# Latent attention of a two-block network: queries and key roots issued one pair ahead, probabilities normalised before the value product

## The chip, the cores and the metric

One core of a Trainium2 chip runs the whole program. The metric is device microseconds of one execution; lower is better. TensorE (PE in the profile) multiplies and writes PSUM, VectorE (DVE) and ScalarE (ACT) read and write both memories, GpSimd (POOL) reads and writes SBUF alone, SyncE (SP) issues the weight transfers.

## What is computed

The reference chains two decoder blocks over 256 tokens of width 1024 (16 meta tokens are put ahead in the first). The first block is a state-space layer, an MLP, a latent attention layer and an MLP; the second has an mLSTM, two cross-attentions, a stick-breaking attention and two gated MLPs. The change lies in the latent attention:

```python
def mla_mixer(h, w_in, q_a_g, w_q_b, kv_a_g, w_kv_b, q_norm_g, k_norm_g, w_out):
    q_lat, kv_lat, k_pe = jnp.split(h @ w_in, [MLA_Q_RANK, MLA_Q_RANK + MLA_KV_RANK], axis=-1)
    q = (rms_norm(q_lat, q_a_g) @ w_q_b).reshape(bsz, L, MLA_HEADS, MLA_QK)
    kv = (rms_norm(kv_lat, kv_a_g) @ w_kv_b).reshape(bsz, L, MLA_HEADS, MLA_NOPE + MLA_V)
    k_nope, v = jnp.split(kv, [MLA_NOPE], axis=-1)
    k = jnp.concatenate([k_nope, jnp.broadcast_to(k_pe[:, :, None, :], ...)], axis=-1)
    q = rms_norm(q, q_norm_g)
    k = rms_norm(k, k_norm_g)
    ...
        sc = jnp.einsum('bqhd,bkhd->bhqk', q[:, s:e], k[:, :e]).astype(jnp.float32) * scale
        mask = jnp.arange(e)[None, :] <= jnp.arange(s, e)[:, None]
        p = jax.nn.softmax(jnp.where(mask, sc, -jnp.inf), axis=-1).astype(v.dtype)
        outs.append(jnp.einsum('bhqk,bkhd->bqhd', p, v[:, :e]))
    o = jnp.concatenate(outs, axis=1).reshape(bsz, L, MLA_HEADS * MLA_V)
    return o @ w_out
```

There are 16 heads with 64 + 32 query and key columns and 64 value columns, a query rank of 384 and a key-value rank of 256; 272 tokens are keys, 256 are queries.

## The kernel before

Each engine has its own program, written out by hand; engines meet only at counting semaphores, which the code names by event (`q.wait_ge(*kw[h])` waits until head h's keys are weighed). Every weight block goes the same way: SP loads it into one of four RAW buffers, ScalarE rounds it to WH, VectorE writes the rest WL = RAW - WH, and TensorE multiplies by both. `PLAN` fixes the order of the blocks for all engines: eight key blocks `wk`, two value blocks `wv`, sixteen query blocks `wqb` (one a head), eight output blocks `mlao`. ScalarE rounds three blocks ahead of its place in the plan (LEAD), VectorE two (LEAD_LO), so a late engine holds back the split of later blocks. A WH and WL buffer is free once the block four back has been used.

Keys stage (`pe_mla`, first loop over c). TensorE makes one 128x272 key block (two heads); VectorE writes both heads' 64 rows to `Kt`, multiplied by the latent root `RKV`; ScalarE squares the block, and `pe_ksum` adds the squares of a head over its rows. VectorE turns the rope part of the keys (`dve_rope_keys`) ahead of the first block, and POOL copies it to all 16 heads in one instruction (`pool_mla`). The token roots of the query latent (`dve_columns(q, "q", ...)`) follow on VectorE in the first block.

Values stage. Six groups of six matmuls of 512 columns, each taken out of PSUM by VectorE (`dve_value`).

Loop over pairs of heads, t = 0 to 10, with `pairs(t)` giving up to four pairs at once: the new pair t (queries, sums of squared queries, key roots), the pair t-1 (scores, row maxima, exponentials), the pair t-2 (probabilities transposed, value product) and t-3 (output transposed back). A key root is a selector times two rows of roots, RKH and RKL, which fills a bank with the root of a head on all partitions; VectorE then multiplies the head's keys by it (`kw`). The value product has the transposed probabilities standing and 64 value columns moving, so its result lies by tokens; VectorE divides it by the row sums (`on`) and TensorE transposes it (`pe_out_transposed`). Only after the last pair do the output blocks `mlao` begin.

## Time and profile before

| | |
|---|---|
| median of 3 runs | 1812.93 us (1812.3 to 1818.2) |
| profiled execution | 1816.08 us, of which the span in the trace is 1814.3 us |
| TensorE busy | 1728.0 us (95%) |
| VectorE, ScalarE, POOL busy | 1193.6, 934.8, 316.0 us |
| latent attention, first key block to last output block | about 534.8 to 699.8 us |

The span of the trace is divided in the page into 40 slices of some 45 us; the latent attention fills slices 12 to 16 (of 1 to 40). Busy matmul time counts overlapping matmuls and matmuls at a lowered clock alike, so the granted clock (PEclk, 1.0 is 2.4 GHz and 0.5 is 1.2 GHz) has to be read beside it.

### The profile page before, as it was taken

What the parts mean: (1) busy time and instruction counts of PE and PEld (TensorE: products, weight loads), DVE (VectorE), ACT (ScalarE), POOL (GpSimd) and SP (SyncE); (2) the same over time, 40 slices, a digit from 0 to 9 for tenths busy, and PEclk for the clock granted to TensorE, in tenths of its full rate; (3) what the DMA queues carried; (4) which work ended last, traced back from release to release, by engine and by line L of the source; (5) the groups of instructions that cost most, each with busy time, mean ns of one, the idle gap of its engine ahead of it and who ended that gap; (6) DMA issues with size and microseconds to landing.
All of it is one profiled execution on the core that took longest, in us unless ns stands there. A gap on an engine that the chain in (4) does not pass through costs nothing.

```text
span 1814.3 us, 33107 instructions
## 1 busy us (share of the span) xinstructions
PE 1728.0 (95%) x13396; PEld 1659.1 (91%) x13396; DVE 1193.6 (66%) x2054; ACT 934.8 (52%) x1640; POOL 316.0 (17%) x281
## 2 busy tenths in 40 slices
PE   6999999999988999999999999999989999989997
PEld 6999889999986989999988999999989998889997
DVE  5899987555576446555766675776666766466665
ACT  5677765544443445544655444544445654354443
POOL 0000001233420002333211100000241211010025
PEclk8999999999998779999999999999999999999998
DMA  5333334555522116555533544455553343335553
GB/s 186 120 114 105 117 103 140 163 176 173 179 79 79 44 57 189 194 187 186 164 116 117 180 146 129 140 183 187 183 169 116 113 156 117 99 123 175 188 179 109
DMA packets 76328, 257.49 MB, mean 142 GB/s; under 512 B 8464, under 2 KB 12560, under 8 KB 75920
## 3 DMA queue, kind: packets, MB, share of 16 engines
q1 hardware_dynamic: 76176, 255.37, 43.9%
q8 instruction: 107, 1.75, 0.4%
q14 instruction: 45, 0.37, 0.1%
HBM read 254.29 MB, written 1.05 MB: 141 GB/s over the span
## 4 chain that ended last, share of the span: by engine, by line
PE 78%; DVE 11%; ACT 5%; issue 4%; POOL 1%; DMA 0%; POOLq 0%; DVEq 0%; ACTq 0%; SPq 0%
PE pb L140 77%; DVE WL L159 2%; DVE TMP L171 2%; DVE SCR L171 2%; DVE SCR L159 2%; PE pb L143 1%; ACT SCR L149 1%; ACT L156 1%; POOL SCR L159 1%; ACT WH L149 1%; DVE HNL L171 1%; ACT TMP L149 1%; ACT Rbuf L149 0%; ACT SCR L150 0%; DVE MX L180 0%
## 5 line engine op out<-in xcount | busy, mean ns | idle before, releaser
L140 PE MATMUL pb<-HNH,WH 128*128 128x256 f32 (+1 forms) x2176 | 632.8, 291 | 3.6 <-DVE WL L159 3.5
L140 PE MATMUL pb<-HNH,WL 128*128 128x256 f32 (+1 forms) x2176 | 621.7, 286 | 0.0
L140 PE MATMUL pb<-HNL,WH 128*128 128x256 f32 (+1 forms) x2176 | 621.2, 285 | 0.0
L159 DVE TENSOR_TENSOR WL<-RAW,WH 128x1024 fp32r<-128x1024 f32 (+4 forms) x514 | 602.5, 1174 | 6.8 <-ACT WH L149 6.1
L149 ACT ACTIVATE WH<-RAW 128x1024 fp32r<-128x1024 f32 (+4 forms) x514 | 507.4, 989 | 170.5 <-PE pb L140 169.0
L140 PE MATMUL pb<-ASH,WH 128*128 128x256 f32 (+1 forms) x1632 | 479.0, 294 | 3.2 <-DVE ASL L171 1.8
L140 PE MATMUL pb<-ASH,WL 128*128 128x256 f32 (+1 forms) x1632 | 469.3, 288 | 0.0
L140 PE MATMUL pb<-ASL,WH 128*128 128x256 f32 (+1 forms) x1632 | 468.8, 287 | 0.0
L140 PEld LDWEIGHTS pb<-HNH,WH 128*128 128x128 f32 x2176 | 415.6, 191 | 10.4 <-issue 4.7
L140 PEld LDWEIGHTS pb<-HNH,WL 128*128 128x128 f32 x2176 | 415.6, 191 | 0.0
L140 PEld LDWEIGHTS pb<-HNL,WH 128*128 128x128 f32 x2176 | 414.2, 190 | 1.1
L140 PEld LDWEIGHTS pb<-ASH,WH 128*128 128x128 f32 x1632 | 315.7, 193 | 10.6 <-issue 5.3
L140 PEld LDWEIGHTS pb<-ASL,WH 128*128 128x128 f32 x1632 | 315.0, 193 | 1.0
L140 PEld LDWEIGHTS pb<-ASH,WL 128*128 128x128 f32 x1632 | 315.7, 193 | 0.0
L140 PE MATMUL pb<-SCR 128*64 128x128 f32 (+11 forms) x928 | 136.2, 319 | 15.5 <-DVE SCR L171 9.5
L140 PEld LDWEIGHTS pb<-SCR 128*128 128x128 f32 (+5 forms) x928 | 105.7, 173 | 36.1 <-DVE SCR L171 11.2
L159 DVE TENSOR_TENSOR ASL<-TMP,ASH 128x256 fp32r<-128x256 f32 (+1 forms) x108 | 46.4, 430 | 109.2 <-ACT ASH L149 109.2
L140 PE MATMUL pb<-SQ,cp 128*128 128x256 f32 (+2 forms) x274 | 85.6, 428 | 33.5 <-ACT SQ L149 24.0
L159 POOL TENSOR_TENSOR SCR<-SCR,TMP 128x256 f32<-128x256 f32 x48 | 59.9, 1248 | 311.7 <-DVE TMP L159 311.7
L159 POOL TENSOR_TENSOR X<-X,TMP 128x272 f32<-128x272 f32 (+1 forms) x64 | 96.4, 1507 | 87.9 <-DVE TMP L159 87.9
L159 DVE TENSOR_TENSOR TMP<-pb,Rbuf 128x256 f32<-128x256 f32 (+1 forms) x112 | 47.9, 428 | 94.8 <-PE pb L140 94.8
L149 ACT ACTIVATE ASH<-TMP 128x256 fp32r<-128x256 f32 (+1 forms) x108 | 45.5, 422 | 117.2 <-DVE TMP L159 67.6
(136 smaller groups left out, 1484.8 us busy)
## 6 DMA issues: line engine op xcount, KB each, us to landing
RAW<-in_w_gu SPq DMA_DIRECT2D x88, 512.0 KB, 4.1
RAW<-in_w_up SPq DMA_DIRECT2D x64, 512.0 KB, 3.5
RAW<-in_w_down SPq DMA_DIRECT2D x64, 512.0 KB, 3.6
RAW<-in_w_ssd SPq DMA_DIRECT2D x48, 512.0 KB, 3.5
RAW<-in_w_xkv SPq DMA_DIRECT2D x32, 512.0 KB, 3.5
RAW<-in_w_mlin SPq DMA_DIRECT2D x24, 512.0 KB, 3.5
RAW<-in_w_fd SPq DMA_DIRECT2D x32, 384.0 KB, 3.0
RAW<-in_w_sbqkv SPq DMA_DIRECT2D x24, 512.0 KB, 3.9
```

The source lines that it names most:

```text
L140: return self.eng.matmul(o, l, r, start=start, stop=stop, skip_group_check=skip) if self.eng else Nothing()
L143: return self.eng.transpose(o, i, ident) if self.eng else Nothing()
L149: return self.eng.activation(o, i, f, bias=bias, scale=scale)
L156: self.eng.preload_act_table_set(name)
L159: return self.eng.tensor_tensor(o, a, b, op) if self.eng else Nothing()
L171: return self.eng.scalar_tensor_tensor(out=o, in0=a, scalar=s, in1=b, op0=op0, op1=op1)
```

## The change

- Plan: the first two query blocks come ahead of the value blocks.
- Keys are no longer multiplied by the latent root when they leave PSUM. One head is copied by VectorE and the other by ScalarE, and the latent root is multiplied into the row of key roots instead. The rope part is multiplied by its inverse (`kpe("inverse")`, `"scaled"`), cut into four steps that stand behind the first four key blocks on VectorE, and POOL copies it in eight pieces, after a 48x272 memset of RKP.
- RKH and RKL become one 48-row tile RKP (rows 0 to 15 and 32 to 47), so a key root is one matmul.
- The loop runs over t = 0 to 7. In one turn TensorE does the scores of pair t, the two query blocks of pair t+1, the transposes of pair t-1, the value product of pair t-2, and the sums and key roots of pair t+1. The sums lie in bank 3 instead of bank 2, so the scores wait for `qss` (they have been read).
- The probabilities are divided by their sums on POOL (`nrm`), 288 and 544 columns a pair, before they are transposed.
- The value product has the values standing and the probabilities moving (256 and 128 columns), and its result lies by features: no `on`, no `pe_out_transposed`.
- PT2 is copied by VectorE instead of ScalarE; PT1 and PT2 have two buffers. The mask is added by one matmul a head instead of two. The row maxima are scaled a head at a time, and so the exponentials of one head start ahead of the other's maxima.
- The last two pairs' transposes and value products are laid between parts of the first three output blocks (`pe_chunks`).

```diff
-    p += [("wk", 0, c) for c in range(8)] + [("wv", 0, k) for k in range(2)]
-    p += [("wqb", 0, h) for h in range(16)]
+    p += [("wk", 0, c) for c in range(8)] + [("wqb", 0, h) for h in range(2)] + [("wv", 0, k) for k in range(2)]
+    p += [("wqb", 0, h) for h in range(2, 16)]
...
         def pe_ksum(q, c):
             if c == 0:
-                q.wait_ge(*rms["kv"])
+                q.wait_ge(*kpe["inverse"])
...
         def pe_scores(q, p):
+            q.wait_ge(*qd[p])
+            q.wait_ge(*qss[p])
...
         def pe_transposed(q, p):
             P = PP[:, p % 2, :]
+            q.wait_ge(*nrm[p])
...
+            q.matmul(o[:, 0:256], vmt[0:32, p, :], PT2[0:32, p % 2, 256:512], True, False, True)
+            for e in range(2):
+                vc = 128 * p + 64 * e
+                q.matmul(o[64 * e:64 * e + 64, 0:256], vtk[:, 0, vc:vc + 64], PT1[:, p % 2, 256 * e:256 * e + 256], False,
+                         False, True)
...
+            for t in range(8):
+                pe_scores(q, t)
+                if t < 7:
+                    pe_query(q, 2 * t + 2)
+                if t:
+                    pe_transposed(q, t - 1)
+                if t < 7:
+                    pe_query(q, 2 * t + 3)
+                if t:
+                    pe_transposed_rest(q, t - 1)
+                if t < 7:
+                    pe_key_root(q, 2 * t + 2)
+                if t > 1:
+                    pe_outputs(q, t - 2)
+                if t < 7:
+                    pe_query_sums(q, t + 1)
+                    pe_key_root(q, 2 * t + 3)
...
+            part(0, 0, 5)
+            pe_outputs(q, 6)
+            part(1, 0, 5)
+            part(0, 5, 6)
+            pe_transposed(q, 7)
+            pe_transposed_rest(q, 7)
+            part(1, 5, 6)
+            part(2, 0, 6)
+            pe_outputs(q, 7)
...
+            for t in range(8):
+                dve_root(q, t)
+                if t > 2:
+                    dve_out(q, t - 3)
+                if t < 7:
+                    dve_block(q, "wqb", 0, 2 * t + 2, T2)
+                else:
+                    dve_split(q, AT["mlao", 0, 0])
+                for e in range(2):
+                    dve_max(q, t, e)
+                if t < 7:
+                    dve_query(q, t + 1)
+                if t:
+                    dve_transposed(q, t - 1)
+                if t < 7:
+                    dve_weigh_key(q, 2 * t + 2)
+                    dve_block(q, "wqb", 0, 2 * t + 3, T2)
+                    dve_weigh_key(q, 2 * t + 3)
+                dve_recip(q, t)
...
         def pool_mla(q):
-            q.wait_ge(*kpe["twice"])
-            q.copy(Kt[64:128, :, :], bc(kpr[64:128, 1, :], 16)).then_inc(*kfill(0))
+            q.mset(RKP[:, :].bitcast(F32), 0.0).then_inc(*rkz(0))
+            q.wait_ge(*kpe["scaled"])
+            for p in range(8):
+                q.copy(Kt[64:128, 2 * p:2 * p + 2, :], bc(kpr[64:128, 1, :], 2)).then_inc(*kfill(p))
+            q.wait_ge(*kfill[7])
+            for p in range(8):
+                P = PP[:, p % 2, :]
+                r = MX[:, p % 2, 12:16].rearrange("p (e n) -> p n e", n=2)
+                q.wait_ge(*rsd[p])
+                for n, (c0, w) in enumerate(SEGS):
+                    d = P[:, 288 * n:288 * n + 2 * w].rearrange("p (e k) -> p e k", e=2)
+                    t = q.tt(d, d, bl(r[:, n, :], w), ALU.mult)
+                t.then_inc(*nrm(p))
```

How the rows move is shown at three places. On TensorE in the loop, from the second query block of a turn to the next scores; L143 rows are transposes, `SCR 128x256`, `64x256` and `64x128` are the value product, `cp,SQ 128x1` the sums of squared queries:

```order
+L143 MATMUL pb<-cp,SCR 128x128 x2
+L143 MATMUL pb<-cp,SCR 32x128 x2
+L140 MATMUL pb<-RKP,RSEL 128x272
+L140 MATMUL pb<-SCR 128x256
+L140 MATMUL pb<-SCR 64x256 x2
+L140 MATMUL pb<-SCR 64x128 x2
 L140 MATMUL pb<-cp,SQ 128x1 x4
-L140 MATMUL pb<-RKH,IDR 128x272
-L140 MATMUL pb<-RKL,IDR 128x272
-L140 MATMUL pb<-SCR 128x128
-L140 MATMUL pb<-SCR 128x64 x2
```

The value product stood behind the sums and a key root; now it stands ahead of the sums, and what follows the sums is one key root (the next row, RKP again) and then the next pair's scores.

On VectorE at the start of the keys stage; `SCR 64x272 <- pb` takes a head's keys out of PSUM, the rows `TMP<-SCR,cp` and `SCR<-SCR,TMP` are rope steps:

```order
+L174 COPY SCR<-pb 64x272
+L171 SCALAR_TENSOR_TENSOR TMP<-pb,Rbuf 64x272
 L165 TENSOR_SCALAR SCR<-SCR,cp 64x272
+L159 TENSOR_TENSOR WL<-RAW,WH 128x256
+L174 COPY SCR<-pb 64x272
 L159 TENSOR_TENSOR TMP<-SCR,cp 32x272
 L159 TENSOR_TENSOR SCR<-SCR,cp 32x272
+L159 TENSOR_TENSOR WL<-RAW,WH 128x256
+L174 COPY SCR<-pb 64x272
 L159 TENSOR_TENSOR SCR<-SCR,TMP 32x272
```

The rope steps stood in one piece ahead of all key blocks; now a split and a copy of a key block stand between them.

On POOL, from the last norm ahead of the layer to the first squares behind it (six of the eight pairs' rows left out):

```order
-L174 COPY SCR<-SCR 64x4352
+L186 MEMSET RKP 48x272
+L174 COPY SCR<-SCR 64x544 x8
+L159 TENSOR_TENSOR SCR<-SCR 128x288
+L159 TENSOR_TENSOR SCR<-SCR 128x544
```

One long copy became eight short ones, and POOL has two multiplications a pair that it did not have.

## Rows read from the trace of the kernel before

**Rows 1.** The page: busy time, and the clock in 40 slices.

```profile
PE 1728.0 (95%) x13396; PEld 1659.1 (91%) x13396; DVE 1193.6 (66%) x2054; ACT 934.8 (52%) x1640; POOL 316.0 (17%) x281
...
PEclk8999999999998779999999999999999999999998
```

**Rows 2.** Windows: each engine's busy time in six stretches of the layer.

```profile
core 0: us, PE busy (x) PEld busy (x) DVE busy (x) ACT busy (x) POOL busy (x), PEclk, DMA share, GB/s
534.79:559.41 24.62, 15.36 (x78) 9.24 (x76) 20.31 (x42) 8.73 (x21) 4.06 (x1) 0.79 0.29 91
559.41:569.27 9.86, 9.86 (x38) 6.38 (x37) 6.74 (x13) 1.82 (x4) 0.00 (x0) 0.83 0.15 42
569.27:579.66 10.39, 8.01 (x50) 7.35 (x49) 5.09 (x13) 3.16 (x8) 0.00 (x0) 0.84 0.24 76
579.66:659.40 79.74, 77.37 (x470) 71.28 (x469) 39.67 (x121) 37.96 (x114) 0.00 (x0) 0.80 0.17 55
659.40:673.08 13.68, 11.67 (x61) 9.98 (x61) 2.92 (x10) 4.28 (x14) 0.00 (x0) 0.75 0.00 0
673.08:699.80 26.72, 26.72 (x202) 26.57 (x201) 15.19 (x24) 13.71 (x23) 3.62 (x3) 0.89 0.47 143
```

**Rows 3.** Waits and timeline, TensorE's longest wait and the rows under it.

```profile
PE pb L140 <- DVE WL L159: 6.1, 1, 6.1
...
539.43 4.06 POOL L174 COPY SCR<-SCR 64x4352 f32<-64x4352 f32 x1 [25.47 <-DVE SCR L174]
...
539.92 3.58 DVE L171 SCALAR_TENSOR_TENSOR TMP<-TMP,SCR 128x2 f32<-128x2 f32 x1
```

**Rows 4.** Timeline: start, duration; a key block and its sum, two value matmuls.

```profile
549.89 0.63 PE L140 MATMUL pb<-SQ,cp 128*16 128x272 f32 x2
550.45 0.39 PE L140 MATMUL pb<-ASH,WH 128*128 128x272 f32 x1
...
566.01 0.40 PE L140 MATMUL pb<-WH,ASL 128*128 128x512 f32 x1
566.25 0.40 PE L140 MATMUL pb<-WL,ASH 128*128 128x512 f32 x1
```

**Rows 5.** Timeline of TensorE in the loop: starts give each part's pace.

```profile
584.70 0.39 PE L140 MATMUL pb<-ASH,WH 128*128 128x256 f32 x1
...
586.93 1.04 PE L143 MATMUL pb<-cp,SCR 128*128 128x128 f32 x8
...
625.15 1.17 PE L140 MATMUL pb<-SCR 128*128 128x128 f32 x8
...
627.35 1.00 PE L140 MATMUL pb<-cp,SQ 96*128 96x1 f32 x8
628.61 0.39 PE L140 MATMUL pb<-RKH,IDR 16*128 16x272 f32 x1 [0.26 <-DVE SCR L159]
...
628.96 2.71 PE L140 MATMUL pb<-SCR 32*128 32x128 f32 x16
631.60 0.59 PE L140 MATMUL pb<-RKH,IDR 16*128 16x272 f32 x1
...
632.34 0.58 PE L140 MATMUL pb<-ASH,WH 128*128 128x256 f32 x1
...
636.35 1.95 PE L143 MATMUL pb<-cp,SCR 128*128 128x128 f32 x10
```

**Rows 6.** Timeline: VectorE in the loop, and POOL beside VectorE elsewhere.

```profile
591.81 0.50 DVE L171 SCALAR_TENSOR_TENSOR SCR<-SCR,cp,pb 128x272 f32<-128x272 f32 x1 [0.60 <-PE pb L140]
...
626.63 0.65 DVE L180 TENSOR_REDUCE SCR<-pb 128x1 f32<-128x144 f32 x2 [1.30 <-PE pb L140]
...
868.79 0.91 POOL L159 TENSOR_TENSOR X<-X,TMP 128x256 f32<-128x256 f32 x1 [0.24 <-DVE TMP L159]
869.03 1.76 DVE L159 TENSOR_TENSOR WL<-RAW,WH 128x1024 fp32r<-128x1024 f32 x1
...
944.13 1.00 POOL L159 TENSOR_TENSOR SCR<-SCR,cp 128x384 f32<-128x384 f32 x1 [2.75 <-ACT SCR L149]
```

More of the change, by code:

```diff
@@ L323, in pe_block, with pe_chunks @@
             q.wait_ge(*lo[i])
+            pe_chunks(q, i, T, xs, 0, KC[name])
+        def pe_chunks(q, i, T, xs, k0, k1):
             o = bank_of(i)[:, 0:T]
-            kc = KC[name]
-            for k in range(kc):
+            kc = KC[PLAN[i][0]]
+            for k in range(k0, k1):
                 xh, xl, ready = xs[k]
@@ new lines, in pe_mla, with part @@
+            ox = as_chunks("o", 8, 8, T2)
+            first = []
+            for m in range(3):
+                first.append(q.block("mlao", 0, m))
+            def part(m, k0, k1):
+                if k0 == 0:
+                    pe_bank_free(q, first[m])
+                    q.wait_ge(*lo[first[m]])
+                pe_chunks(q, first[m], T2, ox, k0, k1)
+            part(0, 0, 5)
[3 more added lines that the diff above has]
+            pe_transposed(q, 7)
@@ L1339, in act_mla @@
                 q.activation(SQ[:, c % 3, 0:T1], b, ACT.Square).then_inc(*eva(i))
+            for e in range(2):
+                act_block(q, "wqb", 0, e, T2)
             act_block(q, "wv", 0, 0, 512)
@@ new lines, in dve_transposed, with dve_recip @@
+        def dve_transposed(q, p):
+            q.wait_ge(*tp2[p])
+            if p > 1:
+                q.wait_ge(*pv[p - 2])
+            q.copy(PT2[:, p % 2, 0:256], banks[6][:, 0:256])
+            q.copy(PT2[0:32, p % 2, 256:512], banks[6][0:32, 256:512]).then_inc(*pt2(p))
+        def dve_recip(q, p):
+            M = MX[:, p % 2, :]
+            q.wait_ge(*ex[2 * p + 1])
+            if p > 1:
+                q.wait_ge(*nrm[p - 2])
+            q.recip(M[:, 12:16], M[:, 8:12]).then_inc(*rsd(p))
@@ L1447, in dve_mla @@
                     dve_columns(q, "kv", 2, 3)
-            dve_rope_keys(q)
+            kv16 = row(RKV, T1)[0:16, :]
             for c in range(8):
                 i, b = dve_block(q, "wk", 0, c, T1)
-                if c == 0:
+                q.wait_ge(*use[i])
+                q.copy(Kt[0:64, 2 * c, :], b[0:64, :]).then_inc(*evd(i))
+                dve_rope_keys(q, c)
+                if c == 5:
                     dve_columns(q, "q", 0, 2)
```

404 lines of the change are left out of this document (195 added, 209 removed), and 2 rows, old and new, of the table _at.

## The prediction

> **What bounds the kernel now.** I read the page first [rows 1]. TensorE is busy for 95% of the span, so time comes back only where it waits or runs at the lower clock. The clock is at 0.9 or more nearly everywhere and falls to 0.7 in two slices; both belong to the latent attention, which is all that the change touches.
>
> The windows [rows 2] divide that layer. In the keys stage (24.62 us) TensorE is busy for 15.36 us while VectorE is busy for 20.31: VectorE sets the pace. The values (9.86) have no gap. The turn into the loop takes 10.39 us. The loop up to the last pair's scores takes 79.74 us, 11.39 a pair, with TensorE busy for 77.37 of it but at a mean clock of 0.80: two fifths of the time at 1.2 GHz, so some 16 us were lost to the clock and only 2.4 to gaps. The last pair's way out takes 13.68 us, the output blocks 26.72, of which the first are slow (0.89).
>
> The list of waits gives the keys stage its reason [rows 3]. TensorE's longest wait there, 6.1 us, is for a split WL. VectorE was late with it, because an operation on two columns took 3.58 us: it began half a microsecond behind POOL's copy of 4352 columns (4.06 us) and ended with it.
>
> The timeline shows one pair's turn [rows 5]. At full clock, scores and masks take 2.20 us (625.15 to 627.35), sums and the wait behind them 1.26, the first key root 0.35, two query blocks 2.23 (584.70 to 586.93). Then the clock has fallen: the value product takes 2.64, the second key root 0.74, the same two query blocks 4.01 (632.34 to 636.35). What came ahead of the fall was sums of one column each, a wait, key roots and a value product of 64 columns a matmul; what came ahead of the rise was four microseconds of dense query blocks. The other pairs' turns look the same.
>
> **Keys, values and the turn into the loop: 44.87 us before, about 31.6 after.** I walk VectorE's new order. TensorE has its first two key blocks done at 536.3, and its first sum now waits for the inverse, which VectorE writes behind its first copy, at about 538.6: 3.8 us from the stage's start. Seven more blocks follow. Each asks of TensorE 0.75 us and a sum of 0.56 [rows 4], of VectorE a split, a copy and a piece of the rope. The sum waits for copy, copy and square in a row on two engines, so I take 1.6 us a block, 11.2 in all. Two query blocks add 2.2 (rows 5 halve to 1.1 each), and the two 1024-column splits for the values come last of all on VectorE, about 1.4 us later than TensorE could use them. POOL's copy now comes in eight pieces of about 0.5 us (4.06 over 8, an estimate from rows 3). If VectorE gets its turn between pieces, four splits wait up to 0.5 us each; I take 1.0 in all. Bounds: 0, since the splits may fall between pieces; 4.1 if POOL lets nobody in before the last piece. Keys stage: 3.8 + 11.2 + 2.2 + 1.4 + 1.0 = 19.6 against 24.62.
>
> Values: 36 matmuls at 0.235 us [rows 4] and a key root of 0.12 are 8.6. The fourth group needs a bank that VectorE empties only after the root sums, a split and the first query pair, which I put 1.1 us late: 9.7 against 9.86, where the first matmuls were at the lower clock. The turn: before, four query blocks of which two were slow, sums, roots. After, sums (1.0), a key root, VectorE's multiplication (0.55 to its start and 0.5 [rows 6]) and the reading of the sums (0.2): 2.3 against 10.39. The queries of pair 1 have moved into the loop, where they are counted. Together 31.6, a gain of 13.3.
>
> **The loop: 79.74 before, about 70.5 after.** At full clock one turn costs TensorE: scores with two masks less, 2.20 - 0.25 = 1.95; two query blocks 2.2; eight transposes 0.9 [rows 5]; two key roots 0.25; sums 1.0. The value product has six instructions of 256 columns and four of 128. A sum of 272 columns is two instructions in 0.56 [rows 4], so 0.26 and 0.13 each are an upper bound, 2.1 in all; I take 2.0. Behind the last key root nothing covers the way to the next scores: VectorE's multiplication begins 0.55 later and takes 0.5, then come reciprocal and reading the sums, 1.3 us together. That wait is new in size: before it was 0.26 behind the sums, and the key root's way was hidden under the value product and the queries. Sum 1.95 + 2.2 + 0.9 + 0.25 + 1.0 + 2.0 + 1.3 = 9.6, and 0.1 for the squares that may be late for the sums: 9.7. Pair 0's turn lacks transposes and product (6.8), pair 1's the product (7.7); five are full (48.5): 63.0.
>
> This is little less than the old loop would take at full clock (79.74 - 16 = 63.7). So the gain hangs on the clock. After sums and wait (2.3 us of hardly any columns) comes a long dense stretch: scores, queries, transposes, queries, a value product that now moves 256 columns. The old stretch of small work was twice as long and took in the value product. I expect a fall in about three turns of five, and only one piece of lowered clock each time. What one costs is read from the query blocks, 4.01 - 2.23 = 1.8 us. 7 turns x 0.6 x 1.8 = 7.5, so 70.5. Bounds: no fall, 63; a fall in each turn twice as long, 3.6 x 7 = 25 more, 88.
>
> **POOL's normalisation** is 832 columns a pair. The nearest row that nothing disturbs multiplies 384 columns in 1.00 us, so about 2.2 us for both. It starts with the reciprocal, 0.3 us ahead of the scores, and TensorE asks for it 1.95 + 1.1 us after their start: just hidden. But it is no free work. Where POOL had begun a two-input operation, a split on VectorE that takes 1.22 elsewhere took 1.76 and ended 1.1 us after POOL was through [rows 6]. So the four small Newton steps of each turn wait for POOL, about 1.5 us; VectorE has some 7 us of work in a turn of 9.7, and the exponentials have slack. I price it at 0.1 a turn. Bounds: 0, and 1.3 us a turn if POOL takes twice as long. The Trainium skill, "GPSIMD Engine Reference", section "4.1 Engine selection", advises VectorE for elementwise work and calls GpSimd about twice as slow with two inputs. By it the edit would be a loss wherever POOL is waited for; the place where it would be is the second rival. The same page's "8. Key points" name contention with VectorE's instructions of two SBUF inputs, which the row of 1.76 us shows.
>
> **The way out: 40.40 before, about 35.9 after.** From the last pair's scores: scores 1.95, wait for POOL's pair 6 about 0.5, transposes 0.9, product 2.0, then 15 output matmuls (1.8), product 2.0, 15 and 3 (2.1), transposes 0.9, 27 (3.2), product 2.0, 12 (1.4): 18.8. Before, TensorE waited some 7 us in this stretch or ran slow. Then the fourth output block's split comes about 1.1 late, since ScalarE rounds it only after the last pair; five blocks of 24 take 14.3; eviction and the feed of the next norm 1.7: 35.9, a gain of 4.5. The edits to masks, PT2's engine and double buffers are in these sums; where they are not on TensorE they are hidden by it.
>
> **Sum.** 13.3 + 9.2 + 4.5 = 27.0. Against the profiled execution that is 1816.08 - 27.0 = 1789.1 us. The median of the runs is 3.15 us lower, so I forecast 1786.
>
> **Rivals.**
> 1. *Forecast*, 1786: chance 0.60. Its own range is 1779 to 1793.
> 2. *POOL is late.* The transposes wait. For it: the reciprocal ends each turn, and POOL must let VectorE's two-input work through. Against it: 2.2 us of work in a 3.3 us gap. At twice the time, 1.3 us in seven turns and the way out, 10 us: 1796. Chance 0.13.
> 3. *The clock stays low longer.* For it: the uncovered wait grew from 0.26 to 1.3 us. Against: dense work on both sides. Two low pieces in each turn make 25.2 us of it instead of 7.5: 1804. Chance 0.13.
> 4. *The long copy's harm stays*, since eight copies follow each other with no wait: 4 us instead of 1, and the clock falls in the values: 1791, inside the forecast's range, with no chance of its own.
> 5. *Better*: falls are rare and VectorE keeps ahead in the keys: 7.5 and 3 us less: 1775. Chance 0.10.
> 6. *Slower than before.* The clock stays low for whole turns, because each now has a gap that it had not. A turn at 1.2 GHz doubles all but the sums and the wait: 7.3 x 2 + 2.3 = 16.9 us. The loop then takes more than 79.74 + 17.8 us from 13.9 a turn on, so it decides when about two thirds of the turns' work is low; all low makes the loop 63 + 7 x 7.2 = 113.4, 33.7 more than before, and the time 1812.93 - 17.8 + 33.7 = 1829. Against it: the old loop rose again in every turn with queries alone. Chance 0.04, a little of it at no change.
>
> **How the numbers follow.** Cases 1, 2, 3 and 5 hold 0.96. The range 1773 to 1801 takes in all of 1 and 5, most of 2 and about half of 3. A measurement of this kernel tells 0.3% (5.4 us) from no change; its three runs span 5.9. Within 0.3% lies only the upper tail of 3 and the lower one of 6, 0.04; slower the rest of 6, 0.04; faster 0.92.
>
> **What would show it.** The scores of pair 0 begin near 566 us instead of 579.7; no VectorE operation of two columns takes over 1 us there. The eight scores follow each other in 9.5 to 11.5 us. TensorE is busy for less than 90% of the loop, with one wait over 1 us a turn, for VectorE's L159 or L171, at a granted clock of 0.87 or more (0.80 before). POOL shows 16 multiplications, about 0.8 and 1.4 us. Output blocks end near 673. I am wrong in the step of the clock if a turn takes more than 12 us with a clock under 0.8, in POOL's step if TensorE's L143 rows wait for POOL, in the keys step if pair 0's scores begin after 571.

## The result, and the profile after

The changed kernel takes 1793.93 us (median of four runs, 1792.79 to 1796.98); the kernel before, run beside it, 1812.91. The ratio is 0.9892, with a 95% interval of 0.9869 to 0.9914: 19.0 us less. The forecast was 1786 in a range of 1773 to 1801, so the direction and the range were right, and the gain came 8 us short. The profiled execution took 1792.79 us (span 1791.0), against 1816.08.

The page of the changed kernel, the rows that answer to [rows 1]:

```profile
PE 1707.4 (95%) x13300; PEld 1634.9 (91%) x13300; DVE 1196.0 (67%) x2065; ACT 933.0 (52%) x1633; POOL 331.2 (18%) x305
...
PEclk8999999999998899999999999999999999989999
```

TensorE is busy for 20.6 us less, and the two slices at 0.7 (14 and 15) read 0.8 and 0.9 now. The windows show where; these five are keys, values, turn into the loop, loop (first scores to last scores) and way out (the last two stretches of [rows 2] in one):

```profile
core 0: us, PE busy (x) PEld busy (x) DVE busy (x) ACT busy (x) POOL busy (x), PEclk, DMA share, GB/s
534.79:555.51 20.72, 16.14 (x97) 10.96 (x96) 16.32 (x40) 12.29 (x30) 5.54 (x8) 1.00 0.37 117
555.51:565.01 9.50, 9.14 (x40) 5.92 (x38) 7.58 (x14) 2.71 (x6) 0.00 (x0) 1.00 0.23 64
565.01:566.98 1.97, 1.26 (x11) 1.07 (x9) 1.32 (x3) 0.15 (x2) 0.00 (x0) 1.00 0.00 0
566.98:643.19 76.21, 68.56 (x392) 58.94 (x393) 45.94 (x135) 34.67 (x102) 10.48 (x13) 0.80 0.18 57
643.19:679.01 35.82, 34.77 (x260) 31.58 (x261) 21.00 (x42) 18.20 (x38) 6.74 (x7) 0.95 0.38 120
```

The longest two-column operations of VectorE in the keys, and the split behind them, beside POOL's eight pieces (5.54 us in the first window above):

```profile
547.41 0.53 DVE L171 SCALAR_TENSOR_TENSOR SCR<-TMP,SCR 128x2 f32<-128x2 f32 x1
547.98 0.55 DVE L159 TENSOR_TENSOR SCR<-SCR 128x2 f32<-128x2 f32 x1
548.45 1.06 DVE L159 TENSOR_TENSOR WL<-RAW,WH 128x384 fp32r<-128x384 f32 x1
```

Keys, values and turn: 32.2 us (forecast 31.6, before 44.87), all of it at full clock. Way out: 35.8 (forecast 35.9, before 40.40). Loop: 76.2 (forecast 70.5, before 79.74), and its granted clock is 0.80 as before. The layer gained 12.7 + 3.5 + 4.6 = 20.8 us; in the profiled execution 2.5 more lie behind the layer.

TensorE's waits from 566 to 645 us, and one turn of the loop on its timeline:

```profile
PE pb L140 <- DVE SCR L159: 6.5, 8, 0.9
PE pb L140 <- ACT SQ L149: 1.9, 2, 1.2
```

```profile
598.61 1.62 PE L140 MATMUL pb<-SCR 128*128 128x128 f32 x8 [0.82 <-DVE SCR L159]
...
603.44 0.60 PE L143 MATMUL pb<-cp,SCR 128*128 128x128 f32 x4
...
604.94 0.60 PE L143 MATMUL pb<-cp,SCR 128*128 128x128 f32 x4
...
605.47 0.39 PE L140 MATMUL pb<-RKP,RSEL 48*128 48x272 f32 x1
605.79 1.50 PE L140 MATMUL pb<-SCR 32*128 32x256 f32 x10
...
607.21 1.05 PE L140 MATMUL pb<-cp,SQ 96*128 96x1 f32 x8
608.20 0.39 PE L140 MATMUL pb<-RKP,RSEL 48*128 48x272 f32 x1
```

The wait that the prediction placed is there, behind the second key root and ahead of the scores: eight times, six of them 0.82 us, the first 0.71 and the last 0.88. The transposes (L143) carry no wait for POOL. The value product lasts from 605.79 to 607.21, 1.42 us. Windows around this turn, and of a later turn up to its second key root (last row), show the clock:

```profile
599.30:602.70 3.40, 3.40 (x14) 3.04 (x14) 3.21 (x10) 0.90 (x5) 0.91 (x1) 0.50 0.07 14
602.70:609.60 6.90, 6.08 (x46) 4.88 (x46) 3.29 (x10) 3.54 (x11) 0.31 (x1) 0.99 0.16 53
609.60:613.00 3.40, 3.40 (x14) 3.10 (x13) 2.98 (x9) 0.89 (x3) 1.40 (x2) 0.50 0.00 0
...
620.17:631.38 11.21, 11.21 (x60) 9.75 (x60) 6.14 (x17) 5.27 (x15) 1.60 (x2) 0.71 0.22 77
```

In this turn, from 0.7 us behind the start of the scores on (ahead of them stand the sums, the second key root and the wait), TensorE is at 0.50 of its clock, the lower of its two levels (1.2 GHz), through the scores and into the query blocks. A fall like it comes in each turn. Windows of 0.2 us show five low stretches of 3.4 us in the loop and two of 6.8, of which the last row holds one (mean 0.71).

### The profile page after: what moved, and what is told of

It reads as the page before. It is cut to its first block, busy times and chain, and to the rows that moved or that the text cites. A ratio compares the mean times of both kernels' runs of the same rounds, so it can differ in the third digit from the quotient of the medians.

```text
span 1791.0 us, 32979 instructions
## 1 busy us (share of the span) xinstructions
PE 1707.4 (95%) x13300; PEld 1634.9 (91%) x13300; DVE 1196.0 (67%) x2065; ACT 933.0 (52%) x1633; POOL 331.2 (18%) x305
## 3 DMA queue, kind: packets, MB, share of 16 engines
HBM read 254.29 MB, written 1.05 MB: 143 GB/s over the span
## 4 chain that ended last, share of the span: by engine, by line
PE 79%; DVE 11%; ACT 5%; issue 4%; POOL 1%; DMA 0%; POOLq 0%; DVEq 0%; SPq 0%; ACTq 0%
PE pb L140 78%; DVE WL L159 2%; DVE TMP L171 2%; DVE SCR L171 2%; DVE SCR L159 1%; PE pb L143 1%; ACT SCR L149 1%; POOL SCR L159 1%; ACT L156 1%; DVE HNL L171 1%; ACT WH L149 1%; ACT TMP L149 0%; ACT Rbuf L149 0%; ACT SQ L149 0%; DVE SCR L165 0%
## 5 line engine op out<-in xcount | busy, mean ns | idle before, releaser
L159 DVE TENSOR_TENSOR WL<-RAW,WH 128x1024 fp32r<-128x1024 f32 (+4 forms) x514 | 603.6, 1175 | 7.7 <-ACT WH L149 7.2
L140 PE MATMUL pb<-ASH,WL 128*128 128x256 f32 (+1 forms) x1632 | 464.6, 285 | 0.0
L140 PE MATMUL pb<-ASL,WH 128*128 128x256 f32 (+1 forms) x1632 | 464.1, 284 | 0.0
L140 PEld LDWEIGHTS pb<-ASH,WH 128*128 128x128 f32 x1632 | 311.6, 191 | 13.2 <-issue 4.9
L140 PEld LDWEIGHTS pb<-ASL,WH 128*128 128x128 f32 x1632 | 310.4, 190 | 1.0
L140 PEld LDWEIGHTS pb<-ASH,WL 128*128 128x128 f32 x1632 | 311.0, 191 | 0.0
L140 PE MATMUL pb<-SCR 128*64 128x128 f32 (+12 forms) x880 | 134.2, 334 | 20.6 <-DVE SCR L171 9.3
L140 PEld LDWEIGHTS pb<-SCR 128*64 128x64 f32 (+6 forms) x880 | 97.9, 172 | 45.5 <-issue 19.3
L159 POOL TENSOR_TENSOR SCR<-SCR 128x512 f32<-128x512 f32 (+2 forms) x36 | 44.6, 1249 | 414.6 <-ACT SCR L149 250.9
L159 DVE TENSOR_TENSOR ASL<-TMP,ASH 128x256 fp32r<-128x256 f32 (+1 forms) x108 | 46.4, 430 | 109.2 <-ACT ASH L149 109.2
L159 POOL TENSOR_TENSOR SCR<-SCR,TMP 128x256 f32<-128x256 f32 x48 | 59.9, 1248 | 312.9 <-DVE TMP L159 312.9
L159 POOL TENSOR_TENSOR X<-X,TMP 128x272 f32<-128x272 f32 (+1 forms) x64 | 96.4, 1506 | 87.9 <-DVE TMP L159 87.9
L159 DVE TENSOR_TENSOR TMP<-pb,Rbuf 128x256 f32<-128x256 f32 (+1 forms) x112 | 47.9, 428 | 94.8 <-PE pb L140 94.8
```

The costliest lines, as they stand in the source:

```text
L140: return self.eng.matmul(o, l, r, start=start, stop=stop, skip_group_check=skip) if self.eng else Nothing()
L159: return self.eng.tensor_tensor(o, a, b, op) if self.eng else Nothing()
```

## The experiments

Twelve kernels were run. To compare loops I take the time from pair 0's first mask matmul to pair 7's (before 80.67 us, changed kernel 76.78) and the windows' mean clock between consecutive ones. "After" stands for the changed kernel. The ratio is always to the kernel before on the same chip.

| kernel | loop, mask to mask, us | mean clock in the loop | median us | ratio, 95% interval |
|---|---|---|---|---|
| after | 76.78 | 0.79 | 1793.93 | 0.9892 [0.9869, 0.9914] |
| key root ahead of the sums | 71.67 | 0.81 | 1791.32 | 0.9882 [0.9866, 0.9898] |
| product last | 73.69 | 0.83 | 1791.85 | 0.9883 [0.9864, 0.9902] |
| filled wait | 70.36 | 0.88 | 1785.75 | 0.9843 [0.9817, 0.9869] |
| no normalisation | 75.59 | 0.81 | 1793.61 | 0.9895 [0.9872, 0.9918] |
| sums woven | 79.35 | 0.81 | 1797.30 | 0.9905 [0.9887, 0.9924] |
| sums between halves | 68.16 | 0.85 | 1788.09 | 0.9857 [0.9843, 0.9872] |
| plain way out | 76.64 | 0.79 | 1796.17 | 0.9906 [0.9893, 0.9919] |
| one copy | 77.02 | 0.79 | 1794.30 | 0.9883 [0.9868, 0.9897] |
| before, pieces alone | 82.48 | 0.77 | 1814.12 | 1.0001 [0.9992, 1.0010] |
| wide sums, order of after | 74.59 | 0.83 | 1792.82 | 0.9881 [0.9865, 0.9898] |
| wide sums between halves | 61.68 | 0.94 | 1781.40 | 0.9811 [0.9794, 0.9828] |
| the same, three gaps filled | 59.37 | 1.00 | 1778.88 | 0.9807 [0.9793, 0.9820] |

### The key root ahead of the sums

```diff
-                    pe_query_sums(q, t + 1)
                     pe_key_root(q, 2 * t + 3)
+                    pe_query_sums(q, t + 1)
```

> The changed kernel with the turn's second key root put ahead of the query sums instead of behind them. Theory A (the loop's missing gain is the clock, and the clock falls because of sums and an uncovered wait in a row): the eight waits of 0.82 us for VectorE's L159 shrink to 0.3 or less, since the key's multiplication now runs under 1.05 us of sums; that alone is 7 x 0.5 to 0.8 = 4 to 5.5 us. If the shorter quiet stretch also keeps the clock up, each turn gives back up to 1.8 us more, and the loop falls from 76 to some 60 to 65 us. Theory B (the quiet one-column sums are enough for the fall, the wait has no part in it): the waits go, the clock still falls in each turn, the loop is 71 to 72 us, the time 4 to 5 us shorter, about 1789. Theory C (VectorE's own chain sets the turn): the wait comes back elsewhere and the time stays at 1793 to 1794.

TensorE's waits in the loop:

```profile
PE pb L140 <- DVE SCR L159: 2.4, 7, 0.3
```

The seven waits of 0.82 to 0.88 became 0.3, and the loop is 5.1 us shorter. But from pair 2 on each turn takes 10.25 us at a mean clock of 0.83: it falls in each, as before. That is theory B's loop. The clock falls without the wait of 0.82 us.

The median moved by only 2.6 us, and the intervals overlap. In the profiled execution the missing part lies behind the layer. The same 8510 matmuls follow in both kernels, here from the end of the layer to the end of the span, after first and then this one:

```profile
679.01:1791.00 1111.99, 1066.58 (x8510) 1034.18 (x8508) 719.27 (x1142) 551.28 (x872) 209.06 (x184) 0.98 0.48 154
```

```profile
673.15:1789.50 1116.35, 1071.61 (x8510) 1039.83 (x8508) 720.49 (x1142) 551.29 (x872) 207.91 (x184) 0.98 0.47 153
```

It takes 4.4 us longer without a change in it. Over all profiled executions this stretch ran from 1111.9 to 1116.5 us. So one profile against another can't judge a layer by the total; the stage's own rows can, and the medians over several runs.

The keys stage varies too. Of the ten profiled executions whose keys stage is that of after, four have it at full clock, and pair 0's first mask comes at 565.7 to 568.1 us. In the other six the clock fell there for 6.8 us, from 540.6 or from 549.6 on, and the mask comes at 568.1 to 572.2. The same stretch, up to pair 0's scores, in the version with wide sums between halves further down:

```profile
534.79:571.05 36.26, 31.30 (x159) 21.26 (x158) 26.46 (x59) 16.14 (x40) 5.55 (x8) 0.91 0.29 84
```

In after it took 32.2 us. A single profile of after shows the better case, and an edit in the loop is best read from mask to mask.

### The product last

```diff
-                if t > 1:
-                    pe_outputs(q, t - 2)
                 if t < 7:
                     pe_query_sums(q, t + 1)
                     pe_key_root(q, 2 * t + 3)
+                if t > 1:
+                    pe_outputs(q, t - 2)
```

> The changed kernel with the value product of the pair before last put at the end of the turn, behind the second key root, where it covers the way from key root over VectorE to the next scores. Theory A: no wait is left in the turn (0.82 us less in seven turns, 5.7 us), and with 1.4 us of product between sums and scores the clock falls in fewer turns; loop 60 to 69 us instead of 76. Theory B (sums alone bring the fall): the waits go, the clock falls still, now perhaps in the product itself; loop 70 to 71 us, time about 1788. Theory C: a wait of about the same size appears ahead of the second key root or the sums, the time stays within 2 us of 1793.9.

```profile
PE pb L140 <- ACT SQ L149: 5.5, 7, 1.2
PE pb L140 <- DVE SCR L159: 1.6, 2, 0.8
```

Theory C's picture in the waits: the wait did not go, it moved. The product had also covered ScalarE's squares, which the sums need; now the sums wait for them, 5.5 us in seven times. The clock still falls: the turns' means are 0.96, 0.84 and then 0.79 to 0.83. The loop is 3.1 us shorter all the same.

### The wait filled

```diff
                     pe_key_root(q, 2 * t + 3)
+                    for _ in range(8):
+                        q.matmul(banks[6][:, 0:240], IDR[:, :], ASH[:, 0, 16:256], True, True, True)
```

> The changed kernel with eight more matmuls of 240 columns each into a bank that nobody reads, behind the second key root of each of seven turns: 0.8 us of dense work at full clock in the place of the uncovered wait; their result is not used. The order of all else stays. Theory A (the idle wait is part of what brings the clock down): the clock stays up through the scores in most turns; the turn loses 1.8 us and the loop is 62 to 68 us. Theory B (sums alone bring it down): the clock falls as before, the extra work runs at the lower clock in part and costs up to 0.8 us a turn more; the loop stays at 76 or grows to 82 us, the time at 1794 to 1799.

```profile
598.95 1.16 PE L140 MATMUL pb<-ASH,IDR 128*128 128x240 f32 x8
599.95 1.17 PE L140 MATMUL pb<-SCR 128*128 128x128 f32 x8
```

Two turns of this version:

```profile
591.81:600.97 9.16, 9.16 (x72) 7.87 (x70) 5.09 (x16) 4.91 (x15) 1.25 (x2) 1.00 0.15 43
600.97:611.51 10.54, 10.54 (x72) 9.12 (x70) 7.91 (x25) 4.80 (x15) 2.19 (x3) 0.87 0.13 39
```

The same turn, with the same work, takes 9.16 us where the clock stays up and 10.5 to 11.1 where it doesn't. Two of the seven turns stayed up, and low stretches are left in five. The loop is 6.4 us shorter although 7 us of useless work were put in. So the wait has a part in the falls, but it isn't all of it. The profiled execution was the slowest of the four (1793.5 us, mean clock 0.972); two took 1781.7 and 1782.3 at 0.981 and 0.980. That more turns stayed up in those is likely, but no trace of them is there.

### No normalisation

POOL multiplies 2 of the 832 columns of probabilities; the rest of the normalisation is left out of the computation.

```diff
-                for n, (c0, w) in enumerate(SEGS):
-                    d = P[:, 288 * n:288 * n + 2 * w].rearrange("p (e k) -> p e k", e=2)
-                    t = q.tt(d, d, bl(r[:, n, :], w), ALU.mult)
-                t.then_inc(*nrm(p))
+                q.tt(P[:, 0:2], P[:, 0:2], r[:, 0, :], ALU.mult).then_inc(*nrm(p))
```

> The changed kernel with POOL multiplying 2 columns of the probabilities instead of 832, so that nearly all of the normalisation is left out of the computation. Theory A and B (POOL is hidden, the clock and the wait set the turn): the transposes did not wait for POOL, but VectorE's small Newton step, held 0.97 us by POOL, comes earlier; that is behind nothing that TensorE asks for: time within 1.5 us of 1793.9. Theory D (POOL's hold on VectorE costs the turn): the waits of 0.82 us for L159 shrink or vanish, 3 to 6 us less, 1788 to 1791.

VectorE's four-column operation that POOL held for 0.97 us takes its 0.16 here (after first, then this version):

```profile
599.26 0.97 DVE L171 SCALAR_TENSOR_TENSOR TMP<-TMP,SCR 128x4 f32<-128x4 f32 x1
...
597.70 0.16 DVE L171 SCALAR_TENSOR_TENSOR TMP<-TMP,SCR 128x4 f32<-128x4 f32 x1
```

TensorE's waits for L159 are still 6.5 us in eight, and the time is that of after (0.9895 against 0.9892). Theory D is out: POOL's normalisation is hidden, and the hold on VectorE costs nothing that can be measured.

### The sums woven into the product

```diff
+                    next(pr, None)
+                    next(pr, None)
                     pe_key_root(q, 2 * t + 3)
+                    for _ in pe_query_sums_parts(q, t + 1):
+                        next(pr, None)
```

Here `pr` gives out `pe_outputs(q, t - 2)` part by part, and `pe_query_sums_parts` the four sums one by one.

> The changed kernel with the turn's second key root after the first two parts of the value product, and the four query sums woven between its other three parts (sum, part, sum, part, sum, part, sum). The runs so far: with the key root ahead of the sums the clock still fell in each of eight turns, but the turn was 0.7 us shorter; with 0.8 us of dense filling in the place of the wait it fell in five. Theory A' (what brings the clock down is the whole quiet stretch, sums and wait together, however it is made up): here no stretch of one-column matmuls is left but a wait of 0.3 to 0.4 us for VectorE ahead of the scores; the sums' loading of weights hides in part behind the product, some 0.5 us less a turn; the clock falls in at most two or three turns; from the first mask to the last the loop takes 60 to 65 us instead of 76.8. Theory B' (a turn has too little dense work whatever its order, or any gap will do): the clock falls in seven or eight turns still, the loop takes 68 to 72 us.

Both theories missed in the profiled execution: the loop is 2.6 us longer than after. It was the slowest of six, which lie at 1790.9 (twice), 1795.0 and 1799.6 to 1801.0, so other executions may have had fewer falls; the median, 1797.3, is no better than after either. The timeline shows work that was added:

```profile
607.64 0.38 PE L140 MATMUL pb<-cp,SQ 96*128 96x1 f32 x2
607.96 0.65 PE L140 MATMUL pb<-SCR 128*64 128x256 f32 x2
608.53 0.38 PE L140 MATMUL pb<-cp,SQ 96*128 96x1 f32 x2
608.85 0.43 PE L140 MATMUL pb<-SCR 128*64 128x128 f32 x2
609.21 0.38 PE L140 MATMUL pb<-cp,SQ 96*128 96x1 f32 x2
```

Two instructions of a sum go by in 0.25 us when sums follow each other (eight in 0.99), but take 0.32 here, and two of 128 columns in the product take 0.36 where ten of the product's instructions take 1.42 together. The weight loads between them stand with idle time for which no other engine is named ("issue"). Product and sums go from 606.11 to about 610.2; that is 4.1, less the key root's 0.31 some 3.8 us, where after needs 2.4 (605.79 to 608.20). Both stretches are at full clock. So I estimate that each change between a matmul of 96 rows and one of 64 output columns costs about 0.2 us (1.4 us over the six or seven more that there are); no run measures one change alone. The Trainium skill, "TensorEngine Tiling (Array Packing)", section "Key Properties", says that a change of tiling mode drains TensorE. The rows can't show a drain, but 3.8 us in place of 2.4 is in line with it.

### The sums between the halves of the product

```diff
-                if t > 1:
-                    pe_outputs(q, t - 2)
+                pr = pe_outputs_parts(q, t - 2) if t > 1 else iter(())
                 if t < 7:
-                    pe_query_sums(q, t + 1)
+                    next(pr, None)
+                    next(pr, None)
+                    next(pr, None)
                     pe_key_root(q, 2 * t + 3)
+                    pe_query_sums(q, t + 1)
+                for _ in pr:
+                    pass
```

> The changed kernel with the second key root and the query sums between the third and fourth part of the value product: the last two parts, some 0.5 us of matmuls of 128 columns, stand between the sums and the next scores, and the sums stay together (1.05 us). Theory A' (sums and wait together): no wait behind the sums, but still 1 us of sums in a row; the clock falls in about half of the turns, as in the filled version, loop 65 to 70 us. Theory B' (falls whatever the order): falls in seven or eight turns, loop 69 to 72 us.

One turn of this version:

```profile
610.48:620.47 9.99, 9.99 (x61) 8.16 (x62) 6.43 (x21) 4.92 (x15) 1.72 (x2) 0.84 0.29 104
```

From pair 2 on TensorE is busy for the whole of each turn, without any wait, and still the clock falls in each (0.91, then 0.84). The loop is 8.6 us shorter than after. TensorE's gaps in it went from 7.65 to 2.8 us (what is left lies in the first two turns), and its mean clock is 0.85 instead of 0.79. The time is 1788.1; the intervals, 0.9857 [0.9843, 0.9872] and 0.9892 [0.9869, 0.9914], overlap by 0.0003, so the gain over after is likely rather than certain. What is left in the turn that could bring the clock down is the sums: 1 us in which TensorE is busy but moves one column an instruction.

### Wide sums, in both orders

```diff
-                    t = q.matmul(banks[3][:, 500 + c:501 + c],
-                                 QSQ[0:96, p % 2, 256 * e + 128 * n:256 * e + 128 * n + 128], cc("ones", 0, 1, 0, 96),
+                    t = q.matmul(banks[3][:, 420 + c:508 + c],
+                                 QSQ[0:96, p % 2, 256 * e + 128 * n:256 * e + 128 * n + 128], cc("ones", 0, 88, 0, 96),
```

The same sum is written to 88 columns; VectorE reads the first.

> The version with the sums between the third and fourth part of the value product, with one edit: each of the four query sums moves 88 columns of ones instead of one, so that the same sum is written 88 times and its first column is read. An instruction of 128 columns takes 1.25 us for eight in the scores, one of a single column 1.05 us for eight, so the sums stay at 1.05 to 1.15 us. Theory S (what brings the clock down is that TensorE moves hardly any columns in the sums, though it is busy with them): the clock now falls in none to three of the eight turns, from the first mask to the last the loop takes 59 to 63 us instead of 68.2, the time is about 1781 to 1784. Theory B'' (TensorE falls in each turn whatever the sums are): seven falls and 68 to 69 us as without the edit, 1788 to 1789.

> The changed kernel as it is, order and waits, with the wide sums alone (88 columns of ones instead of one). Theory S with the sums as the whole cause: falls in none to three turns, loop 65 to 69 us instead of 76.8, time about 1784 to 1787. Theory S+ (sums and the uncovered wait of 0.82 us both count, as the filled version with five falls suggests): falls in four to six turns, loop 70 to 74. Theory B'': eight falls, 77 us, time 1794.

The windows of two turns with the sums between the halves, and the wide sums and what follows them on the timeline:

```profile
591.20:599.73 8.53, 8.53 (x63) 6.91 (x62) 6.00 (x20) 4.79 (x15) 1.72 (x2) 1.00 0.17 46
...
608.26:616.79 8.53, 8.53 (x63) 6.91 (x62) 6.34 (x21) 4.80 (x16) 1.72 (x2) 1.00 0.33 111
```

```profile
614.23 1.12 PE L140 MATMUL pb<-cp,SQ 96*128 96x88 f32 x8
615.28 1.66 PE L140 MATMUL pb<-SCR 128*64 128x128 f32 x12
```

Eight instructions of 88 columns take 1.05 us where eight of one column take 0.98, and with that edit alone the turns went from 10.00 us at 0.84 to 8.53 at 1.00. From pair 2 on there is no fall. One low stretch of 6.8 us is left, from 578.2 on, over the end of the first turn and the start of the second. Falls, loop and time are as theory S expected. The time is 1781.4, ratio 0.9811.

In the order of after the same edit gives 1792.8 (0.9881), no difference that can be told from after. Its first turn and a later one:

```profile
568.15:576.28 8.13, 6.16 (x46) 5.43 (x44) 4.95 (x16) 4.05 (x13) 1.14 (x2) 1.00 0.17 48
597.25:608.49 11.24, 10.42 (x63) 8.74 (x62) 7.06 (x21) 4.93 (x16) 2.16 (x3) 0.81 0.13 36
```

The first turn stays up and takes 8.13 us, the later ones fall (0.89, then 0.79 to 0.81). With the last pair's that makes six falls, within theory S+'s four to six; its loop of 70 to 74 us is missed by 0.6. So neither edit alone keeps the clock up: wide sums with the wait, and sums of one column without the wait, both end in a fall in nearly every turn. Together they keep it up from pair 2 on. In times of the loop: 76.8 with neither, 74.6 with wide sums, 68.2 without waits, 61.7 with both.

### Three gaps filled

The version with wide sums between the halves, with 14 useless matmuls of 240 columns ahead of the first key sum, and 8 ahead of the second key root in the first two turns.

```diff
+                if c == 1:
+                    pe_dense(q, 14, 3)
...
+                    if t < 2:
+                        if t:
+                            q.wait_ge(*pt2[t - 1])
+                        pe_dense(q, 8, 0)
                     pe_key_root(q, 2 * t + 3)
```

> The version with wide sums between the parts of the value product, and dense matmuls whose result nobody reads in three places where TensorE waits: 14 of 240 columns while it waits 1.97 us for the square ahead of the first key sum, and 8 ahead of the second key root in the first two turns, where no value product covers the wait of 0.93 and 1.14 us. Theory S+ (columns per time over sums and waits together bring the clock down): neither the fall of 540.6 to 547.5 nor that of 578.2 to 585.0 us is left; TensorE gets back some 2.5 to 3 us for the latter, and up to the same for the former if TensorE and not VectorE sets the pace of the keys stage; the last pair's mask comes at 627 to 631 instead of 633.8, the time is 1775 to 1779. Rival (those two falls have another cause, or VectorE sets the pace there, and the filling is in the way): 1781 to 1784.

```profile
534.79:568.70 33.91, 30.40 (x155) 21.11 (x153) 24.61 (x54) 15.68 (x39) 5.55 (x8) 0.90 0.29 90
568.70:628.07 59.37, 57.94 (x411) 48.10 (x410) 44.02 (x134) 33.85 (x101) 11.54 (x14) 1.00 0.24 75
```

The loop is at full clock throughout and takes 59.4 us; in the keys one low stretch is left (mean 0.90), from 550.2 on instead of 540.6. As both places and none at all occur without the filling too, what the 14 matmuls do is not shown. Whether this version is better than the one before stays open: 0.9807 [0.9793, 0.9820] against 0.9811 [0.9794, 0.9828].

### The copy in pieces, alone and undone

The first is the kernel before with the fill of the rope rows in eight pieces (pair 0's keys wait for the last of them), the second is after with one copy. The cut is of the first.

```diff
-            q.copy(Kt[64:128, :, :], bc(kpr[64:128, 1, :], 16)).then_inc(*kfill(0))
+            for p in range(8):
+                q.copy(Kt[64:128, 2 * p:2 * p + 2, :], bc(kpr[64:128, 1, :], 2)).then_inc(*kfill(p))
```

> The kernel before, with one edit of the change alone: POOL fills the rope rows of the keys in eight pieces instead of one copy. My prediction's step (the long copy holds VectorE for 3.58 us): the two-column operation takes about 0.6 us, TensorE's wait of 6.1 us in the keys stage falls to about 2.5, and the stage is some 3 us shorter; the values then run at full clock if the wait was what brought it down, 0.5 to 1 us more. Time about 1809. Rival (pieces behind each other without a wait hold VectorE just as long): nothing changes, 1813.

> The changed kernel with POOL's rope fill in one copy again. My prediction's step (the long copy costs up to 4 us and brings the clock down in the values): a VectorE operation of the keys stage takes 3 us or more, pair 0's masks come 2.5 to 4 us later than at 568.1, time 1796 to 1798. Rival (the pieces alone moved the kernel before by nothing): in the changed order nothing on VectorE is urgent beside the copy, the masks come within 1 us and the time is 1793 to 1794.

In the kernel before with pieces, POOL and the two-column operations that follow each other on VectorE:

```profile
538.25 5.41 POOL L174 COPY SCR<-SCR 64x544 f32<-64x544 f32 x8 [25.47 <-DVE SCR L174]
...
538.75 0.41 DVE L171 SCALAR_TENSOR_TENSOR TMP<-TMP,SCR 128x2 f32<-128x2 f32 x1
539.19 0.55 DVE L171 SCALAR_TENSOR_TENSOR SCR<-TMP,SCR 128x2 f32<-128x2 f32 x1
```

```profile
PE pb L140 <- ACT SQ L149: 6.4, 4, 3.3
```

The pieces did what the prediction says: VectorE comes in between them, 0.55 us instead of 3.58. But TensorE's wait of 6.1 us for WL (and 3.1 for ScalarE's squares) became 6.4 for the squares alone, pair 0's masks came 2.8 us earlier, and nothing of it is in the median of ten runs: 1.0001 [0.9992, 1.0010]. In the loop behind it 1.8 us were given back, at a mean clock of 0.77 for 0.79.

In after with one copy, the copy holds a VectorE operation for as long as before:

```profile
545.27 4.07 POOL L174 COPY SCR<-SCR 64x4352 f32<-64x4352 f32 x1 [29.25 <-DVE SCR L171]
...
546.02 3.61 DVE L159 TENSOR_TENSOR SCR<-Rbuf 16x272 f32<-16x272 f32 x1
```

Pair 0's masks are 1.9 us later than in after, less than the 2.5 to 4 expected and less than the 2.4 us between the four executions of after's keys stage at full clock; the time is the same (0.9883 against 0.9892). What is held now is another operation, and TensorE's waits in the keys stage hardly change (4.5 us for the squares instead of 4.2).

### The way out in the old manner

```diff
-            part(0, 0, 5)
             pe_outputs(q, 6)
-            part(1, 0, 5)
-            part(0, 5, 6)
             pe_transposed(q, 7)
             pe_transposed_rest(q, 7)
-            part(1, 5, 6)
-            part(2, 0, 6)
             pe_outputs(q, 7)
             for m in range(3):
-                part(m, 6, 7)
-            for m in range(3):
-                part(m, 7, 8)
+                pe_block(q, "mlao", 0, m, T2, ox)
```

> The changed kernel with the way out in the old manner: transposes and product of the last pairs first, then the eight output blocks one behind the other, no block begun early. My prediction's step (the early blocks cover the waits of the last pair): from the last pair's masks to the last addition to X some 4 to 5 us more than the 34.2 us of the changed kernel, with waits for POOL's normalisation and ScalarE's copies in front of the transposes and the product; time about 1798. Rival (the gain of the way out comes from the clock and the missing transposes of the output, not from the early blocks): within 1 us of the changed kernel there.

```profile
648.83 1.50 PE L140 MATMUL pb<-SCR 32*128 32x256 f32 x10 [1.59 <-DVE ASL L159]
652.28 1.47 PE L140 MATMUL pb<-SCR 32*128 32x256 f32 x10 [0.93 <-DVE SCR L174]
```

Two waits of 2.5 us in all come in front of the products; after has none there, and one of 1.0 us later, for a split. From the last scores on it takes 37.0 us (641.01 to 677.99) instead of 35.8. The blocks begun early are worth 1.2 us in the trace and 2.2 in the medians, whose intervals overlap, not 4 to 5. What the 4.6 are made of is the clock above all: before, 13.68 x 0.25 + 26.72 x 0.11 = 6.4 us of this stretch were lost to it [rows 2], now 35.82 x 0.05 = 1.8. That is 4.6 already; the gaps became 1.0 shorter and the work at full clock 1.0 longer.

## Why the prediction was right, and where it was off

**Keys, values and turn: right.** 20.7, 9.5 and 2.0 us against 19.6, 9.7 and 2.3; together 32.2 against 31.6. No two-column operation of VectorE takes over 0.55 us, and the split behind them 1.06 instead of 0.54, within the 1.0 us that I took. By the windows TensorE's gaps in the three stretches went from 11.6 to 5.65 us. Before, TensorE was busy for 10.7 us at the lower clock there (538.8 to 549.0, 559.2 to 562.6 and 576.4 to 579.7), which cost some 5.4; now for none. That makes 11.4 of the 12.7. The gain did not come from the pieces alone, though: undone in after they are worth 1.9 us of stage time against after's profile and nothing in the median, alone in before nothing. So most of the 12.7 us came with the other edits; that the order did it (queries in the keys' gaps, pair 1's queries moved into the loop) is likely, but was not measured edit by edit. And that the size came out so well is in part luck: in six other executions of the same keys stage the clock fell, and pair 0's scores came up to 4.2 us later.

**The loop: the term of the clock was mis-sized, and it is all of the error.** The busy times and clocks take the loop apart. Lost to the clock: before 79.74 x 0.20 = 15.9 us, after 76.21 x 0.20 = 15.2. Gaps: before 2.4, after 7.65. Work at full clock is the rest: before 61.4, after 53.4. (This takes all of the lower clock's time as work, so it is right to some tenths.) So the change saved 8.0 us of work, gave back 5.3 in waits, and the clock took nearly as much as before. I had the loop at full clock at 63; by these numbers it is 53.4 + 7.65 = 61.0, a little better; the value product took 1.42 us a turn instead of 2.0 and the wait 0.82 instead of 1.3, and a turn that stayed at full clock in the filled version took 9.16 where I had 9.7. The term "7 x 0.6 x 1.8 = 7.5" measured 15.2: the clock fell in each of seven turns, and in two for twice as long (620.17 to 631.38 has a mean of 0.71). The price of a single low stretch was right (3.4 us at half the clock lose 1.7, forecast 1.8); their number was not: counting the two long ones double there were nine, where 7 x 0.6 = 4.2 were forecast. 15.2 - 7.5 = 7.7 us too little there, 2.0 too much in the rest: 5.7, which is the loop's error of 76.2 - 70.5.

The step of reasoning behind it that failed: I took the dense work on both sides of the quiet stretch as speaking for the clock, and held the old loop's longer run of small work to be the reason for its falls. The runs show that the wait or the one-column sums alone mostly suffice: the turns fell with no wait left, and with wide sums but the wait kept; with the wait filled two of seven stayed up. Only with both mended did all turns from pair 2 on stay up, and all seven once the gaps of the first two were filled too. What makes the chip decide so was not measured. The third rival had half of that mechanism (the wait that grew brings the clock down more often) at 1804, the right direction with too high a price.

Of the signs that I had named, pair 0's scores came at 567.0 us (566 forecast), the eight scores followed each other in 9.8 to 11.1 us but for one of 12.2 (620.17 to 632.38, mean clock 0.74), and the loop's clock was 0.80 where I had 0.87 or more. The turn of 12.2 us is my own sign of a wrong step in the clock, met once. The output blocks ended at 679.0, not 673. So the range held although this step failed: the other terms were close, and the error was 5.7 us.

The Trainium skill, "TensorE: Matmul & The Clock Gate", section "HAM oscillation — how this bites in real kernels", tells of a clock that falls again and again in a loop, with waits of several microseconds for transfers as the cause. The falls here came with a wait of 0.82 us, and with none at all (the sums between the halves), so a reader who looks only for long waits would miss them.

**POOL: right.** 1.72 us for both multiplications (2.2 forecast), hidden; without them the time is the same. The advice of the Trainium skill, "GPSIMD Engine Reference", section "4.1 Engine selection", against GpSimd for elementwise work, weighed in the prediction, did not decide here: POOL stood idle for some 9 us ahead of each pair's work.

**The way out: right in size, wrong in the reason.** 35.8 us for 35.9. I had put it to waits covered by early blocks; they are worth 1.2 us in the trace, while the time lost to the clock went from 6.4 to 1.8 us.

**From the sum to the median.** The layer gained 20.8 us, the median 19.0. The profile of before lay 3.15 us above its median and that of after 1.1 below; the stretch behind the layer, which nothing changed, varies by 4.7 us between profiles. So the 8 us that the gain came short are 6.2 in the layer (27.0 - 20.8), less 2.5 gained behind it (within that spread), and 4.3 from where the two profiles lay beside their medians.

## What to carry to other kernels

When a small stage runs at the lower clock, look at what TensorE does just ahead of each fall, and suspect a run of one-column matmuls, which the page counts as busy, as much as a wait. Before taking out a wait, ask what else is quiet beside it: here wide sums alone gave nothing that could be measured, no waits gave 5.8 us, and both together 12.5 more than the change (1793.9 to 1781.4), each edit a few lines. And to move a piece of work out of the place where it covers a wait is to ask for a second wait that it covered too (the squares behind the product).

## What was not expected of the hardware

- A sum of one column and one of 88 columns cost TensorE nearly the same (eight in 0.98 and in 1.05 us), and the eight loads of 128 columns of weights that belong to them took 0.97 us, which is likely the reason. With the sums between the halves of the product, and from pair 2 on, the turns ran at a mean clock of 1.00 with the wider ones and at 0.84 with the others.
- To go back and forth between matmuls of 96 rows and of 64 output columns cost about 0.2 us each time, by an estimate; the woven order took 1.4 us a turn more.
- A stretch of 8510 matmuls that no edit touches took 1111.9 to 1116.5 us from one profile to the next, and a keys stage with the same instructions had a low stretch of 6.8 us in six of ten profiles, in two different places.
- POOL's eight pieces let VectorE in between each two (0.55 us holds), but they took POOL 5.5 us where one copy takes 4.06.
